# Two places in PSUM for the running sum and the token rows of the expert stage

## The reference, cut to what matters

```
hid = gelu(einsum('thkd,td->thk', u_tab[eid], x))     # a dot product per picked expert
y   = einsum('thk,thkd->td', g * hid, v_tab[eid])      # a weighted sum of rows
out = rmsnorm(x_residual + y, final_norm)
```

## Time and profile before

| What | Value |
|---|---|
| Median of three runs | 1687.77 us (1675.85 to 1688.12) |
| Profiled execution, span from first to last instruction | 1709.3 us |
| Expert stage in it | about 640 to 1709 us |
| TensorE, VectorE, ScalarE, GpSimd busy | 82%, 64%, 37%, 38% of the span |
| Mean DMA rate over the span | 389 GB/s |
| Mean granted TensorE clock | 0.956 of full speed |

### The profile page before, as it was taken

One profiled execution on the slowest core, in us unless ns is written; L12 is line 12 of the kernel. 1 busy time (PEld: TensorE's weight loads), 2 busy tenths in 40 slices (PEclk: granted clock), 3 DMA queues, 4 the chain that ended last, 5 costly groups with the idle time before them and its releaser, 6 DMA issues.

```text
span 1709.3 us, 17753 instructions
## 1 busy us (share of the span) xinstructions
PE 1404.9 (82%) x5164; PEld 622.7 (36%) x5164; DVE 1085.5 (64%) x2884; ACT 634.5 (37%) x1889; POOL 652.7 (38%) x703
## 2 busy tenths in 40 slices
PE   8999996768997978888878887777777777777786
PEld 5585663435333434334423232222223222222211
DVE  2459978868000046777766766666668888888654
ACT  2421113445211024344444454444445444444443
POOL 3034333322565653333333333333333333333332
PEclk9999996888998989999999999999999999999999
DMA  9798889999999999999999999999999999999997
GB/s 344 292 357 313 318 318 364 398 411 385 358 362 338 386 375 399 413 409 417 410 423 421 406 416 422 421 421 403 407 422 396 414 422 420 405 419 413 409 406 324
DMA packets 112144, 664.81 MB, mean 389 GB/s; under 512 B 13072, under 2 KB 14336, under 8 KB 52400
## 3 DMA queue, kind: packets, MB, share of 16 engines
q0 software_dynamic: 97824, 571.75, 83.4%
q1 hardware_dynamic: 14224, 91.93, 13.8%
HBM read 658.03 MB, written 5.60 MB: 388 GB/s over the span
## 4 chain that ended last, share of the span: by engine, by line
DMA 37%; PE 37%; issue 8%; ACT 7%; DVE 6%; another core or an unknown queue 3%; POOL 0%; ACTq 0%; SPq 0%; DVEq 0%; POOLq 0%
DMA area_r<-in_uv_tab,eid 36%; PE bank L907 11%; PE bank L627 9%; PE bank L851 4%; PE bank L896 4%; ACT area_c L1003 3%; PE bank L798 2%; DVE area_r L1703 2%; PE bank L558 1%; PE bank L871 1%; ACT L1253 1%; DVE area_x L1711 1%; DMA area_w<-in_w_in 1%; PE bank L767 1%
## 5 line engine op out<-in xcount | busy, mean ns | idle before, releaser
L907 PE MATMUL bank<-area_r,area_c 128*128 128x512 f32 (+1 forms) x1584 | 778.8, 624 | 213.8 <-ACT area_c L1003 212.8
L1873 POOL DMA_INDIRECT area_r<-in_uv_tab,eid x544 | 515.7, 948 | 944.0 <-PE bank L907 590.0
L1703 DVE CUSTOM_DVE_ANT_0 area_r<-area_r,bank 128x1024 f32<-128x1024 f32 x416 | 506.3, 1218 | 288.0 <-DMA area_r<-in_uv_tab,eid 287.3
L907 PEld LDWEIGHTS bank<-area_r,area_c 128*128 128x128 f32 (+1 forms) x1584 | 273.3, 188 | 713.0 <-issue 712.6
L1253 ACT ACTIVATE area_c<-hid 128x1 f32<-128x1 f32 x416 | 84.2, 202 | 538.8 <-DVE hid L1703 538.3
L1694 DVE CUSTOM_DVE_ANT_0 area_r<-area_r,bank 128x1024 f32<-128x1024 f32 x128 | 152.9, 1212 | 25.5 <-DMA area_r<-in_uv_tab,eid 22.7
L627 PE MATMUL bank<-area_w,area_t 128*128 128x384 f32 (+1 forms) x448 | 157.6, 509 | 4.1 <-DMA area_w<-in_w_in 3.5
L1003 ACT ACTIVATE area_c<-ident,area_c 128x128 f32<-128x128 f32 x364 | 146.1, 401 | 34.9 <-ACT area_c L1003 1.1
L1873 POOL DMA_INDIRECT area_r<-in_uv_tab,eidT x128 | 121.4, 948 | 82.0 <-issue 29.3
L1003 ACT ACTIVATE area_x<-bank 128x384 f32<-128x384 f32 (+8 forms) x123 | 49.9, 423 | 212.4 <-remote 59.4
L851 PE MATMUL bank<-area_t,area_w 128*128 128x416 f32 (+1 forms) x448 | 118.8, 418 | 6.1 <-issue 5.2
(11 more groups left out here) (200 smaller groups left out, 1202.6 us busy)
## 6 DMA issues: line engine op xcount, KB each, us to landing
area_w<-in_w_in SPq DMA_DIRECT2D x12, 1536.0 KB, 11.1
area_w<-in_k_cache SPq DMA_DIRECT2D x8, 1920.0 KB
area_w<-in_w_q SPq DMA_DIRECT2D x14, 1024.0 KB, 6.8
area_r<-in_uv_tab,eid POOLq DMA_INDIRECT x544
area_w<-in_w_out SPq DMA_DIRECT2D x4, 2048.0 KB, 11.6
area_w<-in_v_cache SPq DMA_DIRECT2D x4, 1920.0 KB
area_v<-in_v_cache SPq DMA_DIRECT2D x4, 1152.0 KB
area_x<-in_x_p SPq DMA_DIRECT2D x6, 512.0 KB
```

Source lines behind the costliest of these rows:

```text
L907: mm = pe.matmul(acc[0:n, c, :], diag[by_pe(i) % DG][:, 0:n], x_ring[s][:, D + c * 512:D + (c + 1) * 512], start=(i == 0), stop=False, ski ...
L1703: vec.tensor_tensor_reduce(out=u, in0=u, in1=x_cur, scale=1.0, scalar=0.0, op0=ALU.mult, op1=ALU.add, accum_out=hid[t % 2][:, j:j + 1]).th ...
L1873: nc.gpsimd.indirect_dma_start(out=ring[s], out_offset=None, in_=table, in_offset=bass.IndirectOffsetOnAxis(ap=where, axis=0)).then_inc(la ...
```

## The change

The sum and the token rows of a tile get a place by tile: tiles 1 and 3 use banks 0 and 1 as before, tiles 2 and 4 use banks 2 and 3. Six edits follow from it.

- `set_x(t + 1)` moves from the tile's end to the end of group 6 (after slot 111 and its routing). For tile 2 it waits for the last key score.
- `start_sum(t + 1)` moves from before the next tile's slot 0 to after slot 112 of the tile that runs. For tile 2 it waits until the queries have been copied out of bank 2, for tiles 3 and 4 for the y of the tile that used the place before.
- `start_sum(1)`, the residual rows of tile 1, moves from after slot 127 to after slot 96.
- `read_sum` is gone for tiles 1 to 3 (one ScalarE copy each); that of tile 0 stays, as `read_first_sum`.
- `square_y` reads the finished sum in PSUM, at the same slot 5 of the next tile.
- `finish_y` reads it in PSUM too, and writes y to SBUF.

```diff
-        acc = bank[0]
-        x_cur = wide(1, D)
+        SUM_AT, ROWS_AT = {0: 0, 1: 0, 2: 2, 3: 0, 4: 2}, {0: 1, 1: 1, 2: 3, 3: 1, 4: 3}
...
+        REST_AT, NEXT_SUM_AT, NEXT_ROWS_AT = 6 * TOPK, 7 * TOPK, 6
...
             def start_sum(t):
                 n = TILES[t][1]
-                if t >= 2:
-                    pe.wait_ge(acc_read, t)
+                if t == 2:
+                    for c in range(2):
+                        pe.wait_ge(q_copied[c], len(JOBS))
+                if t > 2:
+                    pe.wait_ge(y_ready, t - 1)
                 for c in range(2):
-                    mm = pe.matmul(acc[0:n, c, :], ident[0:n, 0:n], x_tile[t][0:n, c * 512:(c + 1) * 512],
+                    mm = pe.matmul(acc(t)[0:n, c, :], ident[0:n, 0:n], x_tile[t][0:n, c * 512:(c + 1) * 512],
...
-                if t > 1:
-                    start_sum(t)
-                else:
+                if t == 1:
                     pe.wait_ge(acc_read, 1)
...
-                if t == 1:
-                    pe.wait_ge(x_added, len(BY_DVE))
-                    start_sum(1).then_inc(rest_added, 1)
+                    if t == 1 and j == REST_AT:
+                        pe.wait_ge(x_added, len(BY_DVE))
+                        start_sum(1).then_inc(rest_added, 1)
+                    if t < SAMP and j == NEXT_SUM_AT:
+                        start_sum(t + 1)
...
-                if t < SAMP:
-                    read_sum(t)
...
             def set_x(t):
-                if t >= 1:
+                if t == 1:
                     dve.wait_ge(u_free, UR + SLOTS)
-                if t >= 2:
-                    dve.wait_ge(hid_ready, X_END[t - 1])
+                if t == 2:
+                    dve.wait_ge(s_ready, len(SCORED))
+                if t > 2:
+                    dve.wait_ge(hid_ready, X_END[t - 2])
...
-                if t < SAMP:
-                    set_x(t + 1)
+                    if t < SAMP and h == NEXT_ROWS_AT:
+                        set_x(t + 1)
```

More of the change, by code:

```diff
@@ L220, in wide, with acc, x_cur @@
             return bank[i].rearrange("p a b -> p (a b)")[:, 0:n]
-        acc = bank[0]
-        x_cur = wide(1, D)
+        SUM_AT, ROWS_AT = {0: 0, 1: 0, 2: 2, 3: 0, 4: 2}, {0: 1, 1: 1, 2: 3, 3: 1, 4: 3}
+        def acc(t):
+            return bank[SUM_AT[t]]
+        def x_cur(t):
+            return wide(ROWS_AT[t], D)
         x_in = [sem(f"x_in{t}") for t in range(NT)]
@@ L407, in sum_of @@
             n = TILES[t][1]
-            return x_tile[t][0:n, :] if t < SAMP else acc[0:n].rearrange("p a b -> p (a b)")
+            return x_tile[t][0:n, :] if t == 0 else wide(SUM_AT[t], D)[0:n]
+        REST_AT, NEXT_SUM_AT, NEXT_ROWS_AT = 6 * TOPK, 7 * TOPK, 6
         def wait_apart(engine, what, value):
@@ L895, in weigh @@
                 for e in range(2):
-                    mm = pe.matmul(acc[CG * g:CG * g + CG, e, :], wd[g][:, c * CG:c * CG + CG],
+                    mm = pe.matmul(acc(0)[CG * g:CG * g + CG, e, :], wd[g][:, c * CG:c * CG + CG],
                                    v_ring[s][:, e * 512:(e + 1) * 512], start=False, stop=False, skip_group_check=True)
@@ L1265, in weigh_slot, with read_first_sum, square_y @@
                 copy(diag[by_pe(i) % DG][:, 0:TILES[t][1]], eye, w_col[:, j:j + 1]).then_inc(diag_ready, 1)
-            def read_sum(t):
+            def read_first_sum():
+                act.wait_ge(v_free, VR + V_OF[0])
+                copy(x_tile[0], wide(SUM_AT[0], D)).then_inc(acc_read, 1)
+            def square_y(t):
                 n = TILES[t][1]
                 if t == 0:
-                    act.wait_ge(v_free, VR + V_OF[0])
+                    act.wait_ge(acc_read, 1)
                 else:
                     act.wait_ge(x_free, by_pe(X_END[t]))
+                if t == 1:
                     act.wait_ge(rest_added, 1)
-                copy(x_tile[t][0:n, :], acc[0:n].rearrange("p a b -> p (a b)")).then_inc(acc_read, 1)
-            def square_y(t):
-                n = TILES[t][1]
-                if t < SAMP:
-                    act.wait_ge(acc_read, t + 1)
-                else:
-                    act.wait_ge(x_free, by_pe(X_END[t]))
                 nc.scalar.activation(y_junk[0:n, :], sum_of(t), ACT.Square, accum_out=ssq[0:n, t:t + 1]).then_inc(summed, 1)
@@ L1357, in _ @@
             exp_head(HEADS + 1)
-            read_sum(0)
+            read_first_sum()
             for g in range(GROUPS):
@@ L1412, in set_x_first @@
                 dve.wait_ge(squared2, 1)
-                scaled_norm(0, x_cur, x_tile[0]).then_inc(xn_ready, 1)
+                scaled_norm(0, x_cur(0), x_tile[0]).then_inc(xn_ready, 1)
             def norm_h(t):
@@ L1663, in set_x @@
             def set_x(t):
-                if t >= 1:
+                if t == 1:
                     dve.wait_ge(u_free, UR + SLOTS)
-                if t >= 2:
-                    dve.wait_ge(hid_ready, X_END[t - 1])
+                if t == 2:
+                    dve.wait_ge(s_ready, len(SCORED))
+                if t > 2:
+                    dve.wait_ge(hid_ready, X_END[t - 2])
                 if t < SAMP:
-                    ins = vec.tensor_copy(x_cur, xn_tile[t])
+                    ins = vec.tensor_copy(x_cur(t), xn_tile[t])
                 else:
                     for g in range(GROUPS):
-                        ins = vec.tensor_copy(x_cur[g * NSAMP:(g + 1) * NSAMP, :], xn_tile[t][0:NSAMP, :])
+                        ins = vec.tensor_copy(x_cur(t)[g * NSAMP:(g + 1) * NSAMP, :], xn_tile[t][0:NSAMP, :])
                 then(ins)
```

7 lines of the change are left out of this document (3 added, 4 removed).

## The result

The changed kernel took 1689.38 us (median of 22 runs), the kernel before 1687.36 us (median of 22 runs beside it). One run of each, of 6349 and 4693 us, was in a slow state, and no ratio here counts such runs. The ratio is 1.0028 with a 95% interval of 1.0015 to 1.0041, that is 4.7 us slower (2.5 to 6.9). The means of the other 21 runs, 1690.72 and 1685.97 us, are 4.7 us apart too, the medians only 2.0 us. A second job gave 1.0018 (1.0000 to 1.0037), with medians 3.0 us apart. The direction, the rough size and the dear step were right.

What follows compares the result with a forecast made beforehand. It took gathers at the DMA rate, 2.48 us per slot, to bound the expert stage. Terms -4.5 + 4.6 - 0.4 + 6.7 - 1.3 = +5.1 us on 1687.8 gave 1693 us, range 1678 to 1699.

Steps and rivals of the forecast that it cites:

- the dear step: `set_x(4)` after slot 111 of tile 3: four row copies, 4.93 us of VectorE, forecast to lose 6.7 us.
- Part 1: Three tile boundaries: their stalls go, with no sum copied, sum started or rows copied there; -4.5 us.
- Part 2: `square_y` after slot 5: bare stalls in tiles 2 and 4 (+4.6 us), tile 3's slightly cheaper (-0.4 us).
- bare stall: Stall after a square, with no boundary backlog on TensorE to cover it; priced at 2.3 us each.
- free gap: Time between GpSimd's gather issues that loses nothing, about 5.5 us; each us beyond is lost in full.
- Parts 3 and 4: `read_sum` removal, PSUM reads, and earlier `set_x(2)`, `set_x(3)` and `start_sum` of tiles 1 to 3: taken as nothing.
- Part 5: Behind slot 111 of tile 3: `set_x(4)` loses 6.7 us, the samples' Exp stall gives back 1.3 us.
- The samples' Exp: Stall four slots after `set_x(4)`'s event, said to fall into TensorE's backlog: -1.3 us.
- the forecast's own rule: At `set_x(4)`: first issue gap less 5.5 us, plus second gap less 2.5 us, is lost; 6.7 us.
- the half-clock case of 9.4 us: Rival at slot 112: half clock through `start_sum(4)` and slot 113, 9.2 us lost there; total +9.8 us, chance 0.12.

Runs made afterwards that it cites:

- Spread copies: Changed kernel with tile 4's four row copies made one by one after slots 113, 116, 123 and 126 of tile 3; ratio 0.9981 to the kernel before.
- two pieces: Changed kernel with tile 4's four row copies in two pieces, after slots 111 and 118 of tile 3; ratio 1.0007 to the kernel before.
- the one without roots: Changed kernel with y's square root for tiles 1 to 3 replaced by a scaled copy, without its two table loads; ratio 1.0020 to the kernel before.

## Why the prediction came out as it did

**Part 1, the boundaries (-4.5 us): mis-sized.** By the means of the traces the kernel before has an excess of 7.0, 7.7 and 2.5 us in the three stretches with boundaries, the changed one 5.8, 7.5 and 1.3. That is 1.2 + 0.1 + 1.2 = 2.5 us, and it includes what the changed squares do. It leans on the one trace with 7.8 us at the first boundary; by the second trace of before alone it is about 2.0 us, nearly all of it at the third boundary. The failed step is the one that called each byte not moved near a boundary the boundary's own. Part of it is lost there in any kernel, and part is lost once instead of again at the next stall.

**Part 2, the squares (+4.6 - 0.4 us): wrong.** They do become bare and TensorE does idle for 3 us, in tiles 2, 3 and 4 alike. The clock fell in some of them only (in tile 2 in one of two traces, in tile 4 in neither). Without their table loads the kernel is no faster. The failed step is the price of 2.3 us for a bare stall, where the traces show about 0. The price was read from the one row, where the clock had fallen and the rest of a boundary's delay was still to be made up; the gaps in the changed kernel were 5.4, 5.6 and 4.9 us, at the edge of what the free gap covers.

**Parts 3 and 4 (0): right.** The square read PSUM in 1.00 us and finish_y in 1.28 us, where both took 1.04 and 1.28 us from SBUF; keeping the copy changed nothing. The early rows of tiles 2 and 3 leave no gap over 4.3 us at their places.

**Part 5, `set_x(4)` (+6.7 - 1.3 = +5.4 us): right as a whole.** The excess of its stretch went from 0.5 to 6.0 us, +5.5. Idle time (6.26 us), first gap (10.0 us) and the slot at half clock (3.75 us) came as worked out from the rows; the second gap was shorter by 0.8 us, since the clock came back just as the sum started (2.03 us in place of 1.90). Spread copies remove it but for 0.3 us. The two terms are each too large, though. With the measured gaps the forecast's own rule gives (10.01 - 5.5) + (3.88 - 2.5) = 5.9 us in place of 6.7. The samples' Exp did fall into TensorE's backlog, but the whole stretch that holds it had an excess of only 0.6 and 0.4 us before the change, so it had no 1.3 us to give back: again a price taken from a window. The two errors cancel.

The rule itself, all of a gap beyond 5.5 us and behind it all of the next beyond 2.5 us, holds at this place. In the eight traces with a gap over 5.5 us behind slot 111 it gives 5.9, 5.8, 3.1, 4.5, 5.0, 3.8, 5.5 and 9.3 us where the excess is 6.1, 5.9, 2.8, 5.0, 5.1, 3.4, 5.2 and 9.4 us (in the order of the table). It does not hold behind the squares of tile 3, where gaps from none over 4 us up to 6.8 us left the excess of the stretch at 7.2 to 9.0 us in no order.

**The sum.** -2.5 + 5.5 = +3.0 us by the traces (in the sums of the table, 20.7 less 17.6 is 3.1), where the sum said +5.1. The runs say +4.7 (2.5 to 6.9) and +3.0 (0 to 6.2), and the medians +2.0 and +3.0. Parts 1 and 2, -4.5 and +4.2 us, were both far too large, and their sum was off by 2.2 us only (-0.3 against -2.5). That is why the forecast hit: its largest term was right, and the rest was luck. Whether the traces' +3 or the forecast's +5 is nearer to the runs their intervals leave open; how often the half-clock case of 9.4 us comes (one of four traces) is not known, and it would raise the mean of the runs over that of these two traces.

By an estimate from the fixed cost of a DMA in the Trainium skill ("DMA: Bandwidth & Descriptors", the two cost components of a DMA) the free gap would have been about 8 us. The traces do not agree: gaps of 5.4 to 5.6 us cost nothing, one of 7.2 us cost 2 us (two pieces less spread), 10.0 with 3.8 behind it 5.2 us. The 5.5 us taken from the trace fit better.

## What to carry to other kernels

Where a deep queue of transfers is the bound, work taken out of a boundary brings little if the queue had covered most of it, and work put in one piece between two of its users costs all that exceeds the cover: count the largest single hold of each engine, not the sum. An early set-up should go in small pieces, some steps apart (here 1.2 us each, at 0.8 us of spare time per slot), and better not behind another piece that already uses this up. Price a stall by leaving it out in a run, or by the pace of the stage over many steps; the DMA rate in a window of 10 us near it tells too much.

## What the runs showed of the hardware

- TensorE's clock fell from 2.4 to 1.2 GHz while it worked back to back on matmuls over 32 x 32 (twelve records in 7.23 us, 5.7 at full clock; granted clock 0.50 from 1557.8 us on). With eight records over 128 x 128 (3.60 us) and four over 32 x 32 at the same place it stayed at 1.00 until slot 112 ran. One trace each; whether it is the size of the matmuls that counts is not shown.
- After the same idle time of 6.26 us it was back after one slot in both traces of the changed kernel and in the one without roots, and after a slot, the start of a sum and more in a fourth. After the same 2.99 us of idle time in tile 2 it fell in one trace of the changed kernel (0.89 in its window) and not in the other (1.00).
- Every trace loses 5.6 to 6.4 us over the bare cadence in tile 2 (7.8 once), in steps of about 1 us at the same slots in all kernels, near 162, 200, 225 and 249 (as from one dot to the next 3.45 us in place of 2.48 at slot 200 of the changed kernel, counted from tile 1's first). Their cause was not looked into.
